# Inputs laid out in load order, and an eighth FFN slab pair by the seven-product scheme

## The chip, the core and the metric

The kernel runs on one core of one Trainium2 chip. The metric is the device time of one execution in microseconds, the median of several runs. The engines of the core are PE (TensorE; PEld is its weight load), DVE (VectorE), ACT (ScalarE), POOL (GpSimd) and SP (SyncE, which here only issues DMAs). All DMAs share 16 DMA engines.

## What is computed

Two transformer-like blocks in float32 over 256 tokens and a model width of 2048, one after the other. What matters here is the FFN of the second block:

```python
h = rmsnorm_2(x, ffn_norm_g[i])
hid = h @ w_ffn_in[i]                     # 2048 x (2*5632)
gate, up = hid[..., :FFN_HIDDEN], hid[..., FFN_HIDDEN:]
x = x + (jax.nn.silu(gate) * up) @ w_ffn_out[i]
ple = p[i] @ w_ple[i]
x = x + jax.nn.sigmoid(rmsnorm_2(x, ple_norm_g[i]) @ w_ple_gate[i]) * ple
```

Ahead of it stand the first block (projections `w_in`, two recurrent mixers, `w_out`, `w_pg`) and the second block's `w_in_2`, attention, spatial gating and merge. All of them are products of a 256-token activation with weights that are read once, some 400 MB in all.

## The kernel before

**Pieces.** Every weight is cut into slabs of 512 columns and every slab into pieces of 256 rows (`PK = 2` blocks of 128 rows), 512 KB each. A piece g goes through four steps: SP (or POOL) loads it to `raw` (or `ple`, below); ACT copies it to `whi` in the rounded type fp32r; DVE subtracts, `wlo = raw - whi`; PE multiplies. The result has close to float32 accuracy because PE does three products: whi with the high part of the activation, whi with the low part, wlo with the high part. A standard piece is 2 row blocks x 2 token tiles x 3 products = 12 matmuls of 128x512 (lines L1275 for whi, L1280 for wlo), gathered in the PSUM tensor `acc`. `whi` and `wlo` are rings of 4 pieces, so ACT may be at most 4 pieces ahead of PE, and DVE follows ACT. Each engine has its program written out in piece order; `between(g)` puts the small DVE steps behind the split of a certain piece.

**Seven products.** Some pairs of slabs (the gate slab and the up slab j of the FFN, and two pairs of the merge stage) are not done as 2 x 8 standard pieces but as a 2x2 block product over token halves, K halves and the two slabs, by a scheme with seven products M1 to M7 instead of eight. Such a pair is 7 x 4 = 28 pieces of 6 matmuls (L1646 for whi, L1650 for wlo, into `aux`). Its price is on the other engines: every piece is split by ACT (L1097) and DVE (L2458) as a standard one is, though PE works on it for half as long; and eight of the 28 pieces first need a sum of two weight blocks on DVE (`s_sum`, L2453). M5 and M4 need a sum with the four resident pieces of `r1` (in the trace `ple`), which POOL makes by an accumulating DMA (L830): for M5.q once DVE has split M1.q, for M4.q once it has split M6.q. Each block ends in some 512-wide DVE steps: `s_up`, `s_gates` (three), `s_hidden` (three).

**Blocks.** `BLOCKS` is a table: each row is one pair j by seven products, and the standard units that are mixed in (gate or up slabs, or `out`, a slab quarter of the product with `w_ffn_out`). The first two rows belong to the merge stage, the other seven to the FFN (j = 1, 2, 4, 5, 7, 8, 10), each with 16 standard pieces. `add_block` lays them out so that roughly two seven-product pieces stand between two standard ones. `M6.q, M7.q, M3.q` for q = 0 to 3 are in the middle, M4 at the end. `FILLS` says behind which standard piece PE transposes half of a finished hidden slab (4 transposes, L1723); ACT and DVE split it (L1184, L2575) three pieces later. After the last block there is a tail: 16 standard pieces for the hidden slabs 9 and 8, then four times `ple` and two pieces for slab 10, then the last product `gate2` with 32 pieces.

**Loads.** The weights stand in memory as rows of the whole matrix, so a 512-column slab comes in runs of 2 KB. Standard pieces come in pairs of 1 MB (L629, L726), in a seven-product block into two pairs of buffers that take turns: the load of a pair waits for DVE's split of the last piece that stood there. Four slots hold the half loads for the blocks b12, b21, b22 (L743). SP issues all of them in one order, sorted by when the buffer is free.

**Start.** The vectors of gains are loaded as rows and transposed by PE: 16 rows of `norm_w` first (L1298; then DVE copies them, L1856), the rest behind piece 8 (L1304, L1305). `p` and `p_2` (`ptok`, L1258) and the spatial weights `w_s_2` (L1527, from `att_z`) are transposed by PE too, 8 transposes each. PE begins with 8 + 4 throw-away products (`warm`, L1317), between them the first 8 transposes of x.

Of the kernel before, what the change touches and what calls it, by code (L numbers as in the profile page):

```python
# [29 lines left out]
F32 = mybir.dt.float32  # L30
# [68 lines left out]
FILLS = [(0, 2, 0, 0, "d"), (0, 5, 0, 1, "d"), (1, 2, 1, 0, "d"), (1, 5, 1, 1, "d"), (2, 3, 3, 0, "d"), (2, 6, 3, 1, "d"),  # L99
# [12 lines left out]
class Plan:  # L112
# [30 lines left out]
    def unit(self, role, j, q=0):  # L143

        if role == "out":
            return [(role, j, q + i, p) for h in range(2) for i in range(2) for p in (2 * h, 2 * h + 1)]
        return [(role, j, q, p) for p in range(4 if role in ("uA", "uB") else 8)]
# [28 lines left out]
    def plan_ffn(self):  # L176
# [7 lines left out]
        for c in range(M_GROUPS, S_GROUPS):  # L184
# [80 lines left out]
def plan_aux():  # L265

    names = [("gain0", 0)] + [("xT", i) for i in range(8)] + [("gains", 0)]
# [5 lines left out]
    names.extend([("p", 0), ("p2", 0)])  # L273
# [13 lines left out]
    two("tr2", 0); two("ws"); two("tr2", 1); two("tr2", 2)  # L287
# [15 lines left out]
def two_blocks_kernel(nc, A, out):  # L303
# [4 lines left out]
    with ctx:  # L308
# [136 lines left out]
        wsr = zt[:, :, :].rearrange("p a b -> p (a b)")[:, 0:1024].rearrange("p (g s) -> p g s", g=8)  # L445
# [18 lines left out]
        def view(w):  # L464
            return w.rearrange("(k p) n -> p k n", p=P)
# [18 lines left out]
        SHORT = {SLABS[n][0] for q in range(4) for n in (FIRST["DP"] + q, PLAN.ffn_slab["ple", 0, q])}  # L484
        out_k = lambda role, j, p: (4 * j + p * PK) if role == "out1" else 4 * j[p // 2] + p % 2 * PK

        def raw_piece(g):

            slot = PLAN.slot[g] if g >= PLAN.g_plan else g % RAW
            if g not in SHORT:  # L490
                return raw[:, slot]
            pair = raw[:, slot // 2 * 2:slot // 2 * 2 + 2].rearrange("p q k c -> p (q k c)")
            return pair.rearrange("p (k q c) -> p q k c", k=PK, q=2)[:, slot % 2]
# [29 lines left out]
        def s_weights(c, what, q):  # L523
# [31 lines left out]
        hid_of = lambda c: merge_h[c] if c < M_GROUPS else hid_s[c % 2]  # L555
# [63 lines left out]
        def _(sp):  # L619
            piece = [0]  # L620

            def load(src, i=0):
# [6 lines left out]
                sp.dma_start(dst.rearrange("p (k c) -> p k c", k=src.shape[1]), src).then_inc(raw_loaded[g // 2 % (RAW // 2)], 16)  # L629
# [2094 lines left out]
```

## Time and profile before

| | us |
|---|---|
| median of 3 runs (2007.98 to 2010.89) | 2008.88 |
| the profiled execution | 2009.09 |
| its span, from first to last instruction | 2007.4 |
| PE busy | 1997.2 (99%) |
| PE weight load busy | 1663.0 (83%) |
| DVE busy | 1452.3 (72%) |
| ACT busy | 1104.2 (55%) |
| POOL busy | 121.2 (6%) |

The profiled execution lasted 1.7 us longer than its span. Spans of matmuls overlap in the profile (each is shown at 0.39 us, the next begins after 0.23 us), so the share of PE says little by itself: how many matmuls start in a stretch says more. The granted clock is the full 2.4 GHz level throughout by the profile's row of it.

### The profile page before, as it was taken

What the parts mean: (1) busy time and instruction counts of PE and PEld (TensorE: products, weight loads), DVE (VectorE), ACT (ScalarE), POOL (GpSimd) and SP (SyncE); (2) the same over time, 40 slices, a digit from 0 to 9 for tenths busy, and PEclk for the clock granted to TensorE, in tenths of its full rate; (3) what the DMA queues carried; (4) which work ended last, traced back from release to release, by engine and by line L of the source; (5) the groups of instructions that cost most, each with busy time, mean ns of one, the idle gap of its engine ahead of it and who ended that gap; (6) DMA issues with size and microseconds to landing.
All of it is one profiled execution on the core that took longest, in us unless ns stands there. A gap on an engine that the chain in (4) does not pass through costs nothing.

```text
span 2007.4 us, 23490 instructions
## 1 busy us (share of the span) xinstructions
PE 1997.2 (99%) x9253; PEld 1663.0 (83%) x9253; DVE 1452.3 (72%) x1550; ACT 1104.2 (55%) x1373; POOL 121.2 (6%) x116
## 2 busy tenths in 40 slices
PE   9999999999999999999999999999999999999999
PEld 8888888888888888888888888888888888888887
DVE  6877676655666666768787656888888898887664
ACT  6545454554466456555655445656556565665553
POOL 1000000000001100001100000110001100010000
PEclk9999999999999999999999999999999999999999
DMA  8544454556556564558887656889988988887553
GB/s 286 169 146 160 134 181 155 189 188 207 184 184 202 185 211 160 182 195 233 261 231 245 214 189 210 226 252 257 271 257 227 265 243 265 271 227 217 181 194 126
DMA packets 214754, 420.60 MB, mean 210 GB/s; under 512 B 10690, under 2 KB 13428, under 8 KB 214260
## 3 DMA queue, kind: packets, MB, share of 16 engines
q1 hardware_dynamic: 195060, 381.35, 55.5%
q0 software_dynamic: 19584, 37.75, 11.2%
q8 instruction: 73, 1.20, 0.2%
q14 instruction: 37, 0.30, 0.0%
HBM read 414.35 MB, written 4.72 MB: 209 GB/s over the span
## 4 chain that ended last, share of the span: by engine, by line
PE 96%; DVE 1%; DMA 1%; ACT 1%; issue 0%; SPq 0%; DVEq 0%; ACTq 0%
PE acc L1275 48%; PE acc L1280 24%; PE aux L1646 11%; PE aux L1650 6%; PE aux L1258 2%; PE aux L1348 1%; DMA raw<-in_w_ffn_in 1%; DVE wlo L1794 1%; PE aux L1723 0%; ACT whi L858 0%; PE aux L1317 0%; PE aux L1338 0%; PE aux L1249 0%; PE aux L1363 0%; DVE att_z L2296 0%
## 5 line engine op out<-in xcount | busy, mean ns | idle before, releaser
L1794 DVE TENSOR_TENSOR wlo<-raw,whi 128x1024 fp32r<-128x1024 f32 x560 | 681.9, 1222 | 389.1 <-ACT whi L858 379.7
L858 ACT ACTIVATE whi<-raw 128x1024 fp32r<-128x1024 f32 x560 | 591.0, 1059 | 634.2 <-PE acc L1280 550.9
L1275 PE MATMUL acc<-whi,actA_hi 128*128 128x512 f32 x1024 | 404.1, 395 | 1.2 <-ACT whi L858 1.1
L1275 PE MATMUL acc<-whi,actA_lo 128*128 128x512 f32 x1024 | 398.9, 390 | 0.0
L1275 PE MATMUL acc<-whi,actB_hi 128*128 128x512 f32 x860 | 337.5, 392 | 0.0
L1275 PE MATMUL acc<-whi,actB_lo 128*128 128x512 f32 x860 | 334.7, 389 | 0.0
L1280 PE MATMUL acc<-wlo,actA_hi 128*128 128x512 f32 x1024 | 274.1, 389 | 0.0
L1280 PE MATMUL acc<-wlo,actB_hi 128*128 128x512 f32 x860 | 230.4, 390 | 0.7 <-DVE wlo L1794 0.6
L1275 PEld LDWEIGHTS acc<-whi,actA_hi 128*128 128x128 f32 x1024 | 192.3, 188 | 41.0 <-issue 1.6
L1280 PEld LDWEIGHTS acc<-wlo,actA_hi 128*128 128x128 f32 x1024 | 192.2, 188 | 40.3
L1275 PEld LDWEIGHTS acc<-whi,actA_lo 128*128 128x128 f32 x1024 | 192.4, 188 | 38.4
L1097 ACT ACTIVATE whi<-ple 128x1024 fp32r<-128x1024 f32 x144 | 151.2, 1058 | 94.3 <-PE acc L1280 76.4
L2458 DVE TENSOR_TENSOR wlo<-ple,whi 128x1024 fp32r<-128x1024 f32 x144 | 174.0, 1220 | 28.7 <-ACT whi L1097 26.5
L1280 PEld LDWEIGHTS acc<-wlo,actB_hi 128*128 128x128 f32 x860 | 161.3, 188 | 34.9 <-DVE wlo L1794 1.5
L1275 PEld LDWEIGHTS acc<-whi,actB_lo 128*128 128x128 f32 x860 | 161.6, 188 | 32.6
L1275 PEld LDWEIGHTS acc<-whi,actB_hi 128*128 128x128 f32 x860 | 161.5, 188 | 32.7
L1097 ACT ACTIVATE whi<-raw 128x1024 fp32r<-128x1024 f32 x108 | 114.1, 1061 | 88.4 <-PE acc L1280 69.2
L2458 DVE TENSOR_TENSOR wlo<-raw,whi 128x1024 fp32r<-128x1024 f32 x108 | 131.7, 1221 | 36.5 <-ACT whi L1097 33.9
L1646 PE MATMUL aux<-whi,actB_hi 128*128 128x512 f32 x272 | 106.4, 391 | 0.0
L1646 PE MATMUL aux<-whi,actB_lo 128*128 128x512 f32 x272 | 105.9, 389 | 0.0
L830 POOL DMA_DIRECT2D ple<-in_w_ffn_in x56 | 67.7, 1219 | 527.8 <-DVE wlo L2458 501.4
L832 POOL TENSOR_TENSOR rstd<-var,minus_half 128x8 f32<-128x8 f32 (+1 forms) x15 | 24.5, 1631 | 1048.5 <-DVE var L1825 1048.5
(342 smaller groups left out, 2318.6 us busy)
## 6 DMA issues: line engine op xcount, KB each, us to landing
raw<-in_w_in SPq DMA_DIRECT2D x116, 1024.0 KB, 5.0
raw<-in_w_ffn_out SPq DMA_DIRECT2D x44, 1024.0 KB, 7.1
raw<-in_w_ffn_in SPq DMA_DIRECT2D x84, 512.0 KB, 7.7
raw<-in_w_ffn_in SPq DMA_DIRECT2D x32, 1024.0 KB, 6.1
ple<-in_w_ffn_in POOLq DMA_DIRECT2D x56, 512.0 KB, 8.5
raw<-in_w_in SPq DMA_DIRECT2D x32, 512.0 KB, 7.6
raw<-in_w_out SPq DMA_DIRECT2D x16, 1024.0 KB, 4.9
raw<-in_w_pg SPq DMA_DIRECT2D x16, 1024.0 KB, 5.0
```

The costliest lines, as they stand in the source:

```text
L830: pool.dma_start(r1[:, q], s_weights(c, what, q), accum_op=ALU.add).then_inc(sem(f"r1_added{q}"), 16)
L832: pool.tensor_tensor(rstd[:, i, 0:n], var[:, i, 0:n], minus_half[:, 0:n], ALU.pow).then_inc(pow_out, 1)
L858: act.activation(whi[:, g % RING], raw_piece(g), ACT.Copy).then_inc(hi_ready, 1)
L1097: act.activation(whi[:, g % RING], s_source(c, m, q), ACT.Copy).then_inc(hi_ready, 1)
L1258: ins = pe.transpose(bank(u)[:, c * S + t * P:c * S + (t + 1) * P], src[:, t, (c0 + c) * P:(c0 + c + 1) * P], ident[:, :])
L1275: pe.matmul(acc2(n)[:, t, :], act[x][:, k + c, t * P:(t + 1) * P], whi[:, g % RING, c, :], start=(p == 0 and c == 0 and x == 0), stop=False)
L1280: ins = pe.matmul(acc2(n)[:, t, :], act[0][:, k + c, t * P:(t + 1) * P], wlo[:, g % RING, c, :], start=False, stop=(last and c == PK - 1))
L1348: ins = pe.matmul(bank(u)[:, j * m:(j + 1) * m], Kp[n % 2][:, c:c + P], Qp[n % 2][:, j * m:(j + 1) * m], start=True, stop=True)
L1646: pe.matmul(o, lhs(x, q * PK + k), whi[:, g % RING, k, :], start=(q == 0 and k == 0 and x == 0 and not onto), stop=False, skip_group_check ...
L1650: ins = pe.matmul(o, lhs(0, q * PK + k), wlo[:, g % RING, k, :], start=False, stop=(q == 3 and k == PK - 1), skip_group_check=onto)
L1794: dve.tensor_tensor(wlo[:, g % RING], raw_piece(g), whi[:, g % RING].bitcast(F32), ALU.subtract)\
L2458: dve.tensor_tensor(wlo[:, g % RING], s_source(c, m, q), whi[:, g % RING].bitcast(F32), ALU.subtract)\
```

## The change

Two parts. **Layout:** a function on the host, `_lay_out`, hands the weights over as blocks in load order (slab, half of K by 512 rows, partition, 4 row blocks, 512 columns), so that a 1 MB load has one run of 8 KB per partition and a half load one of 4 KB; it also hands over `p`, `p_2`, `w_s_2` and all vectors of gains already transposed, so that PE's transposes and DVE's copies of them go, and 13 small loads become one. **Plan:** the pair 9 is done by seven products as well, so there are eight FFN blocks (j = 1, 2, 4, 5, 7, 8, 9, 10). The standard pieces are dealt out anew: the blocks of 5, 7, 8 and 9 have 12 each instead of 16 (a unit may now be cut by `start` and `stop`), the others 16. The tail loses its 16 `out` pieces and has the four `ple` pieces first. A third hidden buffer, bank "a" for transposes, and waits that match them come with it.

```diff
-    (5, [("out", (3, 2), 0), ("out", (3, 2), 2)]),
-    (7, [("out", (6, 4), 0), ("out", (6, 4), 2)]),
-    (8, [("gate", 9), ("up", 9)]),
-    (10, [("out", (5, 7), 0), ("out", (5, 7), 2)]),
+    (5, [("out", (3, 2), 0), ("out", (3, 2), 2, 0, 4)]),
+    (7, [("out", (3, 2), 2, 4, 8), ("out", (6, 4), 0)]),
+    (8, [("out", (6, 4), 2), ("out", (5, 7), 0, 0, 4)]),
+    (9, [("out", (5, 7), 0, 4, 8), ("out", (5, 7), 2)]),
+    (10, [("out", (8, 9), 0), ("out", (8, 9), 2)]),
...
-        tail = self.unit("out", pair, 0) + self.unit("out", pair, 2) \
-            + [x for q in range(4) for x in (("ple", 0, q, 0), ("out1", last, q, 0), ("out1", last, q, 1))]
+        tail = [("ple", 0, q, 0) for q in range(4)] + [("out1", OUT_LAST, q, p) for q in range(4) for p in range(2)]
...
-        def view(w):
-            return w.rearrange("(k p) n -> p k n", p=P)
+        def chunks(w, c, k, n):
+
+            slab = c // COLS if w != "w_in" or c < MI else (c - HQ) // COLS + MI // COLS
+            return A[w][slab, k // 4, :, k % 4:k % 4 + n, :]
...
-            sp.dma_start(stage1[C_NORM:C_NORM + KD, :], A["norm_w"].rearrange("a (r c) -> (a r) c", c=P))\
-                .then_inc(sem("norm_loaded"), 16)
+            sp.dma_start(gains[:, C_NORM:C_NORM + KD], A["vectors"][:, C_NORM:C_NORM + KD]).then_inc(sem("norm_loaded"), 16)
...
-            pe.wait_ge(sem("norm_loaded"), 16)
-            pe.transpose(bank(0)[:, 0:KD], stage1[0:KD, :], ident[0:KD, 0:KD]).then_inc(aux_full, 1)
...
-                        transposes(("p", 0), ptok[0], 0)
-                        transposes(("p2", 0), ptok[1], 0)
...
-                    if (s, p) == (2, 1):
-                        spatial_weights()
...
-                    if r == "ple" and g == SLABS[m][-1] + 2:
+                    if r == "ple" and g == SLABS[m][-1] + 1:
                         ple_slab(m, x, ple2)
...
+    def blocks(w):
+        k, n = w.shape
+        return w.reshape(k // 512, 4, P, n // COLS, COLS).transpose(3, 0, 2, 1, 4)
```

In the whole program PE has 8944 matmul instructions instead of 8987. Those of 128x512 in split pieces go from 3072 on `acc` with `actA` to 2880, and from 1320 on `aux` to 1488: 24 fewer. 19 transposes go, 8 each of `ptok` and `att_z` and 3 of `stage`. The transposes of the hidden slabs are 88 in both.

At the start of PE's program the kernel before has:

```order
0 L1241 UNCONDITIONAL_BRANCH
1 L1298 MATMUL aux<-ident,stage 128x16
2 L1317 MATMUL aux<-ident 128x128 x8
3 L1258 MATMUL aux<-ident,resid 128x128 x8
4 L1317 MATMUL aux<-ident 128x128 x4
5 L1275 MATMUL acc<-whi,actA_hi 128x512
```

and the changed one:

```order
0 L1230 UNCONDITIONAL_BRANCH
1 L1296 MATMUL aux<-ident 128x128 x8
2 L1247 MATMUL aux<-ident,resid 128x128 x8
3 L1296 MATMUL aux<-ident 128x128 x4
4 L1264 MATMUL acc<-whi,actA_hi 128x512
```

The transpose of `stage`, which waits for the load of `norm_w`, no longer stands ahead of the throw-away products.

In the middle of the block of pair 5 (M6 to M3) the DVE program was as follows; `wlo<-raw` on L1794 is a standard piece, `wlo` on L2458 one of seven products (`ple` as source is M6, `raw` is M7 or M3), L2453 is a sum, L2620 adds a finished `out` slab to the residual:

```order
824 L2458 TENSOR_TENSOR wlo<-raw,whi 128x1024
825 L2453 TENSOR_TENSOR ple<-ple,raw 128x1024
826 L2458 TENSOR_TENSOR wlo<-raw,whi 128x1024
827 L2453 TENSOR_TENSOR raw<-raw 128x1024
828 L1794 TENSOR_TENSOR wlo<-raw,whi 128x1024
829 L2458 TENSOR_TENSOR wlo<-ple,whi 128x1024
830 L2458 TENSOR_TENSOR wlo<-raw,whi 128x1024
831 L2453 TENSOR_TENSOR ple<-ple,raw 128x1024
832 L1794 TENSOR_TENSOR wlo<-raw,whi 128x1024
833 L2458 TENSOR_TENSOR wlo<-raw,whi 128x1024
834 L2453 TENSOR_TENSOR raw<-raw 128x1024
835 L2458 TENSOR_TENSOR wlo<-ple,whi 128x1024
```

The same place in the changed kernel (its lines are L1762, L2416, L2411 and L2578 for the same four things):

```order
818 L2416 TENSOR_TENSOR wlo<-raw,whi 128x1024
819 L2411 TENSOR_TENSOR ple<-ple,raw 128x1024
820 L2416 TENSOR_TENSOR wlo<-raw,whi 128x1024
821 L2411 TENSOR_TENSOR raw<-raw 128x1024
822 L1762 TENSOR_TENSOR wlo<-raw,whi 128x1024
823 L2416 TENSOR_TENSOR wlo<-ple,whi 128x1024
824 L2416 TENSOR_TENSOR wlo<-raw,whi 128x1024
825 L2411 TENSOR_TENSOR ple<-ple,raw 128x1024
826 L2416 TENSOR_TENSOR wlo<-raw,whi 128x1024
827 L2411 TENSOR_TENSOR raw<-raw 128x1024
828 L2578 TENSOR_TENSOR resid<-resid,acc 128x2x512
829 L1762 TENSOR_TENSOR wlo<-raw,whi 128x1024
```

Between two standard pieces there stand now three seven-product pieces with two sums, where there stood two or three pieces with one or two sums; the addition to the residual has moved from between M6.0 and M3.0 to behind M3.1.

On PE, behind the last seven-product block, the kernel before goes on with `out` pieces, among which slab 10 is transposed, and then comes to `ple` (`p1T`). In the changed kernel the end of the block is followed by:

```order
6129 L1264 MATMUL acc<-whi,p1T_lo 128x512
6130 L1269 MATMUL acc<-wlo,p1T_hi 128x512 x4
6131 L1691 MATMUL aux<-ident,hid_std 128x128 x4
6132 L1264 MATMUL acc<-whi,p1T_hi 128x512
6133 L1264 MATMUL acc<-whi,p1T_lo 128x512
```

Slab 10 (`hid_std`) is transposed behind the second and the third `ple` piece, 4 transposes each; in the kernel before such a place among the `out` pieces of the tail was:

```order
6068 L1275 MATMUL acc<-whi,hidT_x_lo 128x512
6069 L1280 MATMUL acc<-wlo,hidT_x_hi 128x512 x4
6070 L1723 MATMUL aux<-ident,hid_s 128x128 x4
6071 L1275 MATMUL acc<-whi,hidT_x_hi 128x512
6072 L1275 MATMUL acc<-whi,hidT_x_lo 128x512
```

## Rows read from the trace of the kernel before

**Rows 1.** The page: busy time and the share of the last chain by engine.

```profile
PE 1997.2 (99%) x9253; PEld 1663.0 (83%) x9253; DVE 1452.3 (72%) x1550; ACT 1104.2 (55%) x1373; POOL 121.2 (6%) x116
...
PE 96%; DVE 1%; DMA 1%; ACT 1%; issue 0%; SPq 0%; DVEq 0%; ACTq 0%
```

**Rows 2.** Waits of PE: engine line waited for, us in total, times, longest.

```profile
PE aux L1298 <- DMA stage<-in_norm_w: 2.5, 1, 2.5
PE acc L1275 <- ACT whi L858: 1.1, 2, 0.9
```

**Rows 3.** PE over time in `gate2`: start, us, line, operation; one standard piece.

```profile
1937.10 0.39 PE L1275 MATMUL acc<-whi,actB_hi 128*128 128x512 f32 x1
...
1939.82 0.39 PE L1275 MATMUL acc<-whi,actB_hi 128*128 128x512 f32 x1
```

**Rows 4.** PE over time at `ptok`, and at the two transposes of gains.

```profile
49.18 1.03 PE L1258 MATMUL aux<-ident,ptok 128*128 128x128 f32 x8
49.98 0.48 PE L1275 MATMUL acc<-whi,actA_hi 128*128 128x512 f32 x1
50.29 0.40 PE L1275 MATMUL acc<-whi,actA_lo 128*128 128x512 f32 x1
```

```profile
36.88 0.27 PE L1304 MATMUL aux<-ident,stage 128*128 128x128 f32 x1
...
37.27 0.50 PE L1275 MATMUL acc<-whi,actA_hi 128*128 128x512 f32 x1
```

**Rows 5.** The start, all engines over time, up to the first product.

```profile
2.08 0.31 ACT L904 ACTIVATE junk<-ident 128x128 f32<-128x128 f32 x1
...
2.72 3.78 PE L1317 MATMUL aux<-ident 128*128 128x128 f32 x16
...
6.30 1.92 PE L1258 MATMUL aux<-ident,resid 128*128 128x128 f32 x8
...
8.21 1.06 ACT L858 ACTIVATE whi<-raw 128x1024 fp32r<-128x1024 f32 x1
...
9.41 0.47 PE L1275 MATMUL acc<-whi,actA_hi 128*128 128x512 f32 x1
```

**Rows 6.** PE where the first two FFN blocks begin; ACT where pair 5's begins.

```profile
1253.19 0.47 PE L1275 MATMUL acc<-whi,actA_hi 128*128 128x512 f32 x1 [0.88 <-ACT whi L858]
...
1341.69 0.50 PE L1275 MATMUL acc<-whi,actA_hi 128*128 128x512 f32 x1 [0.22 <-ACT whi L858]
```

```profile
1506.47 1.06 ACT L858 ACTIVATE whi<-raw 128x1024 fp32r<-128x1024 f32 x1 [5.93 <-DMA raw<-in_w_ffn_out]
```

**Rows 7.** Stretches: PE, PEld, DVE, ACT, POOL busy (instructions), granted clock, DMA share, GB/s.

```profile
1502.00:1585.00 83.00, 83.00 (x371) 68.73 (x370) 71.28 (x66) 49.48 (x51) 9.66 (x8) 1.00 0.89 259
```

**Rows 8.** DVE over time, block of pair 5: M6, M7, M3.

```profile
1536.03 1.22 DVE L2458 TENSOR_TENSOR wlo<-ple,whi 128x1024 fp32r<-128x1024 f32 x1
...
1547.38 1.22 DVE L2458 TENSOR_TENSOR wlo<-ple,whi 128x1024 fp32r<-128x1024 f32 x1
1548.52 1.22 DVE L2458 TENSOR_TENSOR wlo<-raw,whi 128x1024 fp32r<-128x1024 f32 x1
1551.03 1.23 DVE L2453 TENSOR_TENSOR ple<-ple,raw 128x1024 f32<-128x1024 f32 x1 [1.30 <-DMA raw<-in_w_ffn_in]
...
1555.58 1.22 DVE L2458 TENSOR_TENSOR wlo<-ple,whi 128x1024 fp32r<-128x1024 f32 x1
```

**Rows 9.** PE over time: the two wlo products of M6.2 in that block.

```profile
1557.79 0.61 PE L1650 MATMUL aux<-wlo,actB_hi 128*128 128x512 f32 x2
```

**Rows 10.** POOL over time in that block, and its eight DMAs to landing.

```profile
1513.63 2.45 POOL L830 DMA_DIRECT2D ple<-in_w_ffn_in  x2 [0.97 <-DVE wlo L2458]
```

```profile
DMA to landing us min/median/max: 5.8/8.5/15.5
```

**Rows 11.** The page: DMA queues, SP's (q1) and POOL's (q0); packets, MB, share of 16 engines' span.

```profile
q1 hardware_dynamic: 195060, 381.35, 55.5%
q0 software_dynamic: 19584, 37.75, 11.2%
```

More of the change, by code:

```diff
@@ L141, in __init__, with unit @@
             assert free < need
-    def unit(self, role, j, q=0):
+    def unit(self, role, j, q=0, start=0, stop=8):
         if role == "out":
-            return [(role, j, q + i, p) for h in range(2) for i in range(2) for p in (2 * h, 2 * h + 1)]
+            return [(role, j, q + i, p) for h in range(2) for i in range(2) for p in (2 * h, 2 * h + 1)][start:stop]
         return [(role, j, q, p) for p in range(4 if role in ("uA", "uB") else 8)]
@@ L265, in plan_aux @@
 def plan_aux():
-    names = [("gain0", 0)] + [("xT", i) for i in range(8)] + [("gains", 0)]
+    names = [("xT", i) for i in range(8)]
     def two(name, *key):
@@ L348, in two_blocks_kernel @@
         rs = ExitStack()
-        stage1 = sb("stage1", [P, P], at=rs)
-        stage2 = sb("stage2", [C_END - P, P], at=rs)
-        ptok = [sb(f"ptok{n}", [P, T, PE_DIM], at=rs) for n in range(2)]
+        sb("fill_stage", [P, 256], at=rs)
+        p_raw = [sb(f"p_raw{n}", [P, PK, S], at=rs) for n in range(2)]
         rs.close()
@@ L489, in raw_piece @@
             slot = PLAN.slot[g] if g >= PLAN.g_plan else g % RAW
[L490 to L493, printed above, removed]
+            return raw[:, slot]
         S_SRC = {"M1": None, "M2": "b21", "M5": None, "M6": None, "M7": "b12", "M3": "b22", "M4": None}
@@ L526, in s_weights @@
             w, col = s_columns(c, 0 if what in ("b11", "b21") else 1)
-            return view(w[0])[:, k:k + PK, col:col + COLS]
+            return chunks(w, col, k, PK)
         def s_columns(c, half):
             j = BLOCKS[c][0] * COLS
-            return (A["w_in_2"], (GA2, GB2)[half] + j) if c < M_GROUPS else (A["w_ffn_in_2"], (FFN, 0)[half] + j)
+            return ("w_in_2", (GA2, GB2)[half] + j) if c < M_GROUPS else ("w_ffn_in_2", (FFN, 0)[half] + j)
         def s_done(eng, c, m):
@@ L577, in filled, with fill_place @@
             eng.wait_ge(sem("tr_taken"), 1 + [x[2:4] for x in FILLS].index((j, h)))
+        def fill_place(f):
+            c, _, _, _, b = FILLS[f]
+            return 2 if b == "d" else 3 - own(c)
         def fill_bank(f):
-            c, _, _, _, b = FILLS[f]
-            return aux[:, 2 if b == "d" else 3 - own(c), :].rearrange("p (c s) -> p c s", c=2)
+            return aux[:, fill_place(f), :].rearrange("p (c s) -> p c s", c=2)
         def fill_dst(x, f):
@@ L1715, in fill @@
                 else:
-                    pe.wait_ge(sem("tr_taken"), f)
+                    same = [x for x in range(f) if fill_place(x) == fill_place(f)]
+                    if same:
+                        pe.wait_ge(sem("tr_taken"), same[-1] + 1)
                 if b == "e":
                     pe.wait_ge(sem("s_up"), c + 1)
+                elif b == "a":
+                    pe.wait_ge(sem("hid_odd_ready"), c)
                 else:
@@ L2629, in between @@
                 for (role, j, q), n in PLAN.ffn_slab.items():
-                    if role == "out" and j != OUT_TAIL[0] and g == SLABS[n][-1] + (2 if SLABS[n][-1] in PLAN.block_end else 3):
+                    if role == "out" and g == SLABS[n][-1] + (2 if SLABS[n][-1] in PLAN.block_end else 3):
                         out_added(n, q)
```

155 lines of the change are left out of this document (65 added, 90 removed), and 6 rows, old and new, of the table FILLS.

## The prediction

> **What bounds the kernel now.** I read the page first: PE is busy 99% of the span and is 96% of the chain that ended last [rows 1]. Such a share can hide gaps, so I looked at PE's waits: apart from the first, they come to some 2 us [rows 2]. Where nothing but standard pieces run, a piece starts every 2.72 us, 226.7 ns for each of its 12 matmuls [rows 3]; nearly the whole span has that spacing. So PE's instructions are the time: what leaves PE is gained, unless the others fall behind. DVE's 72% is an average; in the FFN blocks it is 71.28 of 83 us, and the DMA engines are at 0.89 [rows 7]. There the slack is small, and the change makes exactly this part denser.
>
> **Matmuls.** The instruction lists have 24 fewer matmuls of 128x512: 192 go (16 standard pieces), 168 come (28 pieces of 6). 24 x 0.2267 = **-5.44 us** on the path.
>
> **Transposes.** Eight of `ptok` start at 49.18, the next matmul at 49.98 and its successor 0.31 later instead of 0.23 [rows 4]: 0.80 + 0.08, say 0.9 us. The eight of `att_z` are of the same shape: 0.9. The two of gains take 0.39 up to the next matmul [rows 4], with the same 0.1 behind: 0.5. Sum **-2.3 us**. What goes with them on DVE and ACT lay under PE's work and gives nothing. The masking of the spatial weights stays on POOL, and they are needed seven slabs later.
>
> **Start.** PE's first instruction waits 2.5 us for the load of `norm_w` [rows 2]; then come the throw-away products, and the x transposes start behind them without a gap [rows 5]. The identity was ready by 2.08, when ACT read it [rows 5]; ACT had just loaded its table, so it may have been ready some tenths earlier. Without the wait PE can begin 0.6 to 1.0 us earlier, and the chain transposes, ACT, DVE, first product at 9.41 [rows 5] moves along as far as x and the first weights have landed. Bounds: 0 if one of these is late, -1.0 if none is. ACT took up the first weights at 8.21 with no wait in its row, so I take **-0.8**.
>
> **Loads.** One run of 8 KB instead of four of 2 KB. The trace has no weight load in such runs, so the gain in rate is at least nothing; from above nothing bounds it, and I take 5%. It matters in two ways. At the start of the first FFN block PE stood 0.88 us for a late load and at that of the second 0.22 [rows 6]; both should mostly go: **-1.0** (bounds 0 and -1.4, the two with their slower restart). And it pays for the denser blocks: a copy costs 0.555 x 16 x 2007.4 / 381.35 = 46.7 engine-us per MB, 2.9 us on 16 engines, an accumulation 0.112 x 16 x 2007.4 / 37.75 = 95, or 6.0 us [rows 11]. A block of 16 standard pieces has 32 copies and 8 accumulations of 0.524 MB, 49 + 25 = 74 us of 83, which is the 0.89 of [rows 7]. A block of 12 has 28 copies: 43 + 25 = 68 us in 28 x 1.36 + 12 x 2.72 = 71 us: 0.95 at the old rates, 0.92 if copies are 5% faster.
>
> The Trainium skill speaks against a gain in rate ("DMA: Bandwidth & Descriptors", Specifications): 512 B are enough for line rate, and the old runs are four times that. By it the term -1.0 would be 0 and the 0.95 would hold; that is the second case below. No run here shows yet which is right.
>
> **The four dense blocks (pairs 5, 7, 8, 9).** On average DVE keeps up: 40 splits + 8 sums + up to 2 additions to the residual, at 1.135 us from start to start (1547.38, 1548.52 in [rows 8]) are 57 us, some nine or ten 512-wide steps at about 0.7 another 6: 63 of 71. But in the middle (M6 to M3) three seven-product pieces and one standard piece are 3 x 1.36 + 2.72 = 6.80 us of PE and 4 splits + 2 sums = 6.81 us of DVE: no slack at all for four rounds. Before, that stretch had 1.33 standard pieces a round: 7.7 us of PE against 7.2 of DVE. DVE lives there on the lead that it brings. In the block of pair 5 the split of M6.2 ended at 1555.58 + 1.22 = 1556.80, PE wanted it at 1557.79 [rows 8, 9]: a lead of 1.0 us, after an idle 1.3 us for a half load. The order of DVE up to M6.2 stays nearly the same, so the dense block arrives there with about the same lead, and now two rounds without recovery follow, with the addition to the residual (1.135 us) behind M3.1 in the blocks of 5 and 8; those of 7 and 9 have none between M6.0 and M7.3. I get some 1.0 us of PE standing in block 5, 0.6 in block 8 (a split of transposes more, but PE's own transposes too), about none in 7 and 9.
>
> Second, the sums for M5 come by accumulating DMAs. The last of block 5 was issued near 1514.9 and landed 15.5 us later, at 1530.4; DVE split M5.3 at 1536.03, ACT 1.1 us before [rows 8, 10]. So it had 4.5 us to spare; from M1.3 to M5.3 a dense block is 5.44 us of PE shorter (16.32 for 21.76). DVE then waits about 1 us and brings less lead to M6. That costs another 0.2 to 0.5 us a block. Third, at every block's beginning the third standard piece waits for its load: ACT stood 5.93 us for it and went on at 1506.47 [rows 6], just in time. This distance stays 8.16 us of PE or more, so 0 to 0.3 a block. Together **+2.5 us**, bounds 0 and 7. The blocks of 1, 2, 4 and 10 keep the old density and cost nothing new.
>
> **Tail.** 16 pieces that gave DVE a rest go; slab 10 is transposed behind the second and third `ple` piece, 5 us after its block, when DVE's hidden step (three 512-wide operations, some 2 us) is done. The split of its second half may be some 0.2 us late; that lies inside the bounds above.
>
> **Sum.** 2009.09 - 5.44 - 2.3 - 0.8 - 1.0 + 2.5 = 2002.05 for an execution like the profiled one; that one stood 0.2 above the median of the runs, so **2001.9 us**.
>
> **The rivals.**
> 1. *The layout gives no rate.* Then -1.0 goes, and in the dense blocks the DMA engines stand at 0.95. For it: 259 GB/s with a share of 0.89 [rows 7] tells of accumulations, not of short runs. Against it: fewer, longer packets. Price: +1.0, and about 1 us more in each dense block: 2001.9 + 1 + 4 = 2007. Chance 0.12.
> 2. *Slower: accumulations starve in the dense blocks.* Both queues share the 16 engines; if a turn of SP's queue carries up to four times the bytes of before, POOL's gets a smaller part. Place: M5.3. From the split of M1.3 (3.8 us ahead of PE by the order of the pieces) to PE's need are 16.3 + 3.8 us; ACT and DVE take 2.3, which leaves 17.8 for the DMA, now up to 15.8 with its wait. It decides from there: landing at 21.3 stops PE 3.5 us in every dense block and leaves DVE no lead for the middle, which is worth 1.5 more: 4 x 5 = 20 in place of 2.5, some 2019. Against it: the four accumulations have few copies beside them that are not needed anyway. Chance 0.06.
>    The Trainium skill (same page, "Queues, rings and completion order") has the engines take turns between queues packet by packet; by it this shift is possible, and no row of the kernel before can show it.
> 3. *DVE never runs out*, and the start gives its full 1.0: 2009.09 - 5.44 - 2.3 - 1.0 - 1.0 - 0.2 = 1999.2. It is the good end of the forecast.
> 4. *The change does not do what it says*: the dense blocks are bound by DVE, so that the 5.44 are eaten. Against it: 63 of 71 us on average; it would take stops of over 1.4 us in each of them beyond what I counted: 2007 to 2009. Chance 0.05.
>
> **How the numbers follow.** Forecast 0.75 (1999.2 to 2004.8, with the good end), rival 1 0.12, rival 2 0.06, rival 4 0.05, something else 0.02. A measurement of this kernel can tell about 0.2%, 4.0 us, from no change: faster is below 2004.9, slower above 2012.9. Faster 0.77, same 0.16, slower 0.07. The range leaves out rival 2 and the far parts of 1 and 4: 1999.0 to 2007.0.
>
> **What would show it.** Right: in the profile after, 43 fewer PE instructions, the first product near 8.6, matmuls 226.7 ns apart outside the dense blocks, PE's waits of 1 to 2 us in the middle of the blocks of 5 and 8 with DVE `wlo` as the releaser, no wait at the start of the first FFN block, SP's queue below 55.5% of the span. Wrong: PE waits for `ple` loads at M5 or M4 (rival 2), a DMA share of 0.95 in the dense blocks (rival 1), PE waits in all four of them (rival 4), or first weights that land after 8.5.

## The result, and the profile after

The changed kernel takes 2013.44 us (median of 20 runs, 2009.77 to 2017.07), the kernel before 2009.62 (20 runs): ratio 1.0021, 95% interval 1.0015 to 1.0027. It is slower by 0.2% (3.8 us) where the prediction said 2001.9 and faster. The profiled execution took 2013.15, its span is 2011.6 against 2007.4.

From the page of the changed kernel, the rows that answer to [rows 1] and [rows 11]:

```profile
PE 1994.4 (99%) x9210; PEld 1655.0 (82%) x9210; DVE 1473.1 (73%) x1569; ACT 1115.5 (55%) x1386; POOL 103.5 (5%) x124
...
q1 hardware_dynamic: 66080, 381.35, 51.7%
q0 software_dynamic: 11520, 41.95, 12.0%
...
PE 85%; DMA 6%; DVE 6%; ACT 1%; issue 1%; SPq 0%; ACTq 0%; DVEq 0%
```

43 PE instructions fewer, as the lists said, and SP's queue needs less of the DMA engines. But PE's share of the last chain fell from 96% to 85%: DMAs and DVE now end it, each for 6%. PE's waits (engine line waited for, us in total, times, longest), which answer to [rows 2]:

```profile
PE aux L1614 <- DVE wlo L2416: 3.2, 3, 1.3
PE acc L1264 <- ACT whi L846: 2.6, 3, 1.7
PE acc L1269 <- DVE wlo L1762: 2.3, 3, 0.8
```

**Where they are.** The 1.7 is the start's, one 1.3 stands at 954 us, a 0.6 at 809 was there before; nearly all the rest is in the four dense blocks or right behind them. The last matmul of the program ended in the kernel before at 2002.16 + 0.39, its first product of the block of pair 5 began at 1502.48; in the changed kernel:

```profile
1501.64 0.39 PE L1264 MATMUL acc<-whi,hidT_x_hi 128*128 128x512 f32 x1
```

```profile
2006.24 0.39 PE L1280 MATMUL acc<-wlo,actB_hi 128*128 128x512 f32 x1
```

Up to the block of pair 5 the changed kernel is 0.84 us ahead (1502.48 - 1501.64). From there to PE's end it needs 504.99 us where the other needed 500.07. With 24 matmuls fewer it should be 494.6, so it loses **10.4 us** there. I had put 2.5. Counted from the trace as what the starts of neighbouring matmuls are apart over the usual 0.23 us, some 5.5 of it stand in the middle of the four blocks, 1.7 at M4.3, 1.7 at the third standard piece of the next block and 0.5 at the start of `gate2`, where PE waits 0.17 us for DVE's split of the activation; the rest is short gaps.

**The first kind of stop**, DVE in the middle of the block of pair 5, where [rows 8, 9] showed a lead of 1.0 us:

```profile
1545.01 1.23 DVE L2411 TENSOR_TENSOR ple<-ple,raw 128x1024 f32<-128x1024 f32 x1 [1.18 <-DMA raw<-in_w_ffn_in]
1546.15 1.22 DVE L2416 TENSOR_TENSOR wlo<-raw,whi 128x1024 fp32r<-128x1024 f32 x1
1547.29 1.22 DVE L2411 TENSOR_TENSOR raw<-raw 128x1024 f32<-128x1024 f32 x1
1548.42 1.22 DVE L2578 TENSOR_TENSOR resid<-resid,acc 128x1024 f32<-128x1024 f32 x1
1549.55 1.22 DVE L1762 TENSOR_TENSOR wlo<-raw,whi 128x1024 fp32r<-128x1024 f32 x1
```

```profile
1550.83 1.21 PE L1269 MATMUL acc<-wlo,hidT_x_hi 128*128 128x512 f32 x4 [0.84 <-DVE wlo L1762]
```

DVE waits 1.18 us for a half load, works without a gap behind it, and PE stands when the split of 1549.55 is not there in time. There is no slack between two standard pieces, so nothing makes the wait good: what it and the addition to the residual (1.13 us) come to beyond DVE's lead, PE stands. In the block of pair 7 there is no addition, and the half loads alone do it (DVE waits 0.71 us for one and 2.63 for the next):

```profile
1628.28 1.23 DVE L2411 TENSOR_TENSOR ple<-ple,raw 128x1024 f32<-128x1024 f32 x1 [2.63 <-DMA raw<-in_w_ffn_in]
```

```profile
1630.69 0.50 PE L1614 MATMUL aux<-wlo,actB_hi 128*128 128x512 f32 x1 [1.11 <-DVE wlo L2416]
```

The block of 8 has a half-load wait of 1.37 us, that of 9 two of 1.28 and 1.79. In the kernel before, each block had one such wait of 1.30 to 1.37 us and one of 0.4 or less, and PE stood behind none of them. **The second kind** closes the block. ACT at M4.3 and at the third standard piece of the next block, and the chain of work through the first of them (start, us, what):

```profile
1569.27 1.06 ACT L1086 ACTIVATE whi<-ple 128x1024 fp32r<-128x1024 f32 x1 [4.81 <-DMA ple<-in_w_ffn_in]
...
1579.02 1.06 ACT L846 ACTIVATE whi<-raw 128x1024 fp32r<-128x1024 f32 x1 [4.62 <-DMA raw<-in_w_ffn_out]
```

```profile
1559.38 9.87 DMA ple<-in_w_ffn_in
1569.25 0.02 issue
1569.27 1.07 ACT whi L1086
1570.34 0.02 issue
1570.36 1.24 DVE wlo L2416
1571.60 0.04 issue
1571.64 0.73 PE aux L1614 x2
```

The accumulating DMA for M4.3 can start only when DVE has split M6.3. It took 9.87 us, and PE followed at once. ACT waits for this DMA in all four dense blocks; PE stops for it in those of 5 and 7, in the second trace (e11) also in that of 9.

**DVE and the DMA engines over a dense block** (PE, PEld, DVE, ACT, POOL busy, granted clock, DMA share, GB/s), which answers to [rows 7]:

```profile
1502.00:1575.00 73.00, 71.77 (x313) 57.82 (x312) 63.19 (x59) 43.91 (x45) 6.90 (x8) 1.00 0.83 247
```

DVE's 63.19 us are what I had counted (63 of 71), and the DMA share did not rise to 0.92: it fell to 0.83. Neither average was the bound.

### The profile page after: what moved, and what is told of

Same layout as the page of the kernel before. It is cut to its first block, busy times and chain, and to the rows that moved or that the text cites. A ratio compares the mean times of both kernels' runs of the same rounds, so it can differ in the third digit from the quotient of the medians.

```text
span 2011.6 us, 23458 instructions
## 1 busy us (share of the span) xinstructions
PE 1994.4 (99%) x9210; PEld 1655.0 (82%) x9210; DVE 1473.1 (73%) x1569; ACT 1115.5 (55%) x1386; POOL 103.5 (5%) x124
## 3 DMA queue, kind: packets, MB, share of 16 engines
q1 hardware_dynamic: 66080, 381.35, 51.7%
## 4 chain that ended last, share of the span: by engine, by line
PE 85%; DMA 6%; DVE 6%; ACT 1%; issue 1%; SPq 0%; ACTq 0%; DVEq 0%
PE acc L1264 45%; PE acc L1269 22%; PE aux L1610 9%; PE aux L1614 4%; DVE wlo L2416 2%; DMA raw<-in_w_ffn_in 2%; DMA ple<-in_w_ffn_in 2%; PE aux L1247 2%; PE aux L1327 1%; DVE wlo L1762 1%; DMA raw<-in_w_ffn_out 1%; DMA raw<-in_w_in 1%; DVE ple L2411 1%; DVE raw L2411 1%; ACT whi L1086 0%
## 5 line engine op out<-in xcount | busy, mean ns | idle before, releaser
L1762 DVE TENSOR_TENSOR wlo<-raw,whi 128x1024 fp32r<-128x1024 f32 x544 | 662.8, 1223 | 399.5 <-ACT whi L846 391.7
L1264 PE MATMUL acc<-whi,actA_hi 128*128 128x512 f32 x960 | 379.3, 395 | 1.7 <-ACT whi L846 1.7
L1264 PE MATMUL acc<-whi,actA_lo 128*128 128x512 f32 x960 | 374.7, 390 | 0.0
L1269 PE MATMUL acc<-wlo,actA_hi 128*128 128x512 f32 x960 | 257.4, 390 | 0.0
L1086 ACT ACTIVATE whi<-ple 128x1024 fp32r<-128x1024 f32 x160 | 167.2, 1058 | 99.9 <-PE acc L1269 54.2
L2416 DVE TENSOR_TENSOR wlo<-ple,whi 128x1024 fp32r<-128x1024 f32 x160 | 193.3, 1221 | 27.4 <-ACT whi L1086 25.3
L1264 PEld LDWEIGHTS acc<-whi,actA_hi 128*128 128x128 f32 x960 | 180.6, 188 | 38.5 <-issue 2.2
L2416 DVE TENSOR_TENSOR wlo<-raw,whi 128x1024 fp32r<-128x1024 f32 x120 | 145.9, 1221 | 24.7 <-ACT whi L1086 22.0
L1610 PE MATMUL aux<-whi,actB_hi 128*128 128x512 f32 x304 | 119.0, 391 | 0.0
L1610 PE MATMUL aux<-whi,actB_lo 128*128 128x512 f32 x304 | 118.3, 389 | 0.0
L1614 PE MATMUL aux<-wlo,actB_hi 128*128 128x512 f32 x304 | 94.2, 391 | 2.1 <-DVE wlo L2416 1.9
L818 POOL DMA_DIRECT2D ple<-in_w_ffn_in x64 | 55.3, 864 | 586.9 <-DVE wlo L2416 564.5
```

The lines of the kernel that those rows point to most:

```text
L818: pool.dma_start(r1[:, q], s_weights(c, what, q), accum_op=ALU.add).then_inc(sem(f"r1_added{q}"), 16)
L1086: act.activation(whi[:, g % RING], s_source(c, m, q), ACT.Copy).then_inc(hi_ready, 1)
L1264: pe.matmul(acc2(n)[:, t, :], act[x][:, k + c, t * P:(t + 1) * P], whi[:, g % RING, c, :], start=(p == 0 and c == 0 and x == 0), stop=False)
L1269: ins = pe.matmul(acc2(n)[:, t, :], act[0][:, k + c, t * P:(t + 1) * P], wlo[:, g % RING, c, :], start=False, stop=(last and c == PK - 1))
L1610: pe.matmul(o, lhs(x, q * PK + k), whi[:, g % RING, k, :], start=(q == 0 and k == 0 and x == 0 and not onto), stop=False, skip_group_check ...
L1614: ins = pe.matmul(o, lhs(0, q * PK + k), wlo[:, g % RING, k, :], start=False, stop=(q == 3 and k == PK - 1), skip_group_check=onto)
```

## Experiments

The base is the changed kernel unless said otherwise. "Over 494.6" is the stretch from the first product of the block of pair 5 to PE's end, less the 494.6 us that its matmuls and transposes need; it comes from one trace of each kernel, the ratios from 5 to 11 executions of each against the kernel before. It is more than the sum of the waits that the profile names, since PE starts again more slowly (from 1549.59 to 1550.83 above are 1.24 us, 1.01 more than the usual 0.23, for a wait of 0.84), and it holds a stretch at half clock in e4 and three in e6 (last section). The profiled executions of e1 and e9 have one more right behind their first product. e4 and e8 leave out a part of the computation, as their texts say.

| kernel | ratio, 95% | over 494.6 |
|---|---|---|
| changed kernel | 1.0021 (1.0015 to 1.0027) | 10.4; again: 14.8 |
| e1 layout, old plan | 0.9988 (0.9979 to 0.9997) | (old plan) |
| e2 plan, old layout | 1.0018 (1.0010 to 1.0027) | 7.1 |
| e3 dense blocks spread anew | 0.9974 (0.9966 to 0.9983) | 4.8 |
| e4 no sums on DVE | 0.9986 (0.9977 to 0.9995) | 8.2 |
| e5 as e3, first slab in 2 KB runs | 0.9978 (0.9969 to 0.9986) | 6.4 |
| e6 as e3, spread otherwise | 1.0038 (1.0025 to 1.0050) | 17.2 |
| e7 as e3, all inputs in the old layout | 0.9981 (0.9973 to 0.9990) | 3.4 |
| e8 plain copies on POOL's queue | 0.9996 (0.9987 to 1.0006) | 9.2 |
| e9 as e3, weights in 2 KB runs | 0.9969 (0.9956 to 0.9981) | 1.5 |
| e10 as e3, middle as before | 0.9996 (0.9987 to 1.0005) | 6.0 |

**e1 and e2: the two parts apart.** e1 is the diff without its hunks on `BLOCKS`, `FILLS`, `HID_T`, the tail and the transposes' banks; e2 is those hunks alone.

> The new layout and the transposed inputs with the plan of before (seven FFN blocks of 16 standard pieces, 16 out pieces in the tail). Theory A, the plan makes the stops: the blocks of 16 run without stops as before, the 19 transposes (-2.3) and part of the late loads (-0.5 to -1.0) are gained, and the one new stop at 954 (1.5 us, a half load that landed 3.2 us later than before) may come back: 2006 to 2008, ratio 0.998 to 0.999. Theory B, runs of 4 and 8 KB make the half loads and the accumulations land later wherever both queues are busy: stops of 1 us or more appear in the old blocks too, time 2010 or more, ratio 1.000 to 1.003.

> The new plan (eight FFN blocks, four of them with 12 standard pieces) with the inputs as before in runs of 2 KB. Theory A: 24 matmuls less (-5.4), but the stops of the four dense blocks stay at 9 us or grow, since the DMA engines carry the same bytes: 2013 to 2016, ratio 1.001 to 1.003. Theory B: the dense blocks stop for 2.5 us or less as they should have by my count: 2005 to 2008, ratio 0.998 to 0.999.

e1: 2007.44 us, e2: 2013.33, before 2009.53. So the plan alone is as slow as the whole change (theory A): its own four dense blocks stop wherever the inputs lie, and the blocks of 16 in e1 have no stop of over 0.2 us. But the layout, worth 0.12% by itself, brought nothing that shows on top of the plan (1.0018 and 1.0021, each known to some 0.1%), although 19 transposes went with it. So something of it may cost in the dense blocks what the transposes gave.

**e3: deal the 12 pieces out anew.**

```diff
-            upto = max(0, min(28, (t - 1) * 28 // (len(std) - 3)))
+            upto = (0, 3, 6, 9, 12, 14, 16, 19, 21, 24, 28, 28)[t] if len(std) == 12 else max(0, min(28, (t - 1) * 28 // (len(std) - 3)))
```

> The changed kernel with the 12 standard pieces of a dense block dealt out otherwise: behind the 2nd one come three seven-product pieces at once (before: behind the 3rd), and one more stands between M6 and M3. Theory A1, stops come where the pieces of PE are too short for DVE (M6 to M3) and where four standard pieces in a row share two pairs of buffers (the block's beginning): the stops of the four blocks fall from 9.4 us to 3 or less, 2005 to 2008. Theory A2, the accumulating DMAs for M4.3 and M5.3 are the bound, since they land 0.02 us before ACT takes them: these two places are as far from their source as before, so the stops only move there, 2011 to 2014.

2004.12 us: seven changed table entries are worth 0.47%, 9.4 us, and the kernel beats both. The same work, DMAs and bytes are there. PE's waits in it (the first row is the start's 2.4 and one of 0.7 at a block's beginning; the 0.7 of the second stands in the middle of the block of 9, behind a half load that DVE waited 3.29 us for):

```profile
PE acc L1264 <- ACT whi L846: 3.1, 2, 2.4
PE aux L1614 <- DVE wlo L2416: 0.7, 1, 0.7
PE aux L1610 <- ACT whi L1086: 0.5, 1, 0.5
```

**e10 parts e3's two moves.** `(0, 3, 6, 9, 12, 15, 18, 21, 24, 26, 28, 28)`. It is not e3's first move alone: M6.3 to M4.3 has two standard pieces here, where e3 and the changed kernel have one.

> The kernel of e3 without its additional standard piece between M6 and M3 (every third place again, as in the changed kernel); it now stands between M4.1 and M4.2, and three pieces are still behind the 2nd at the block's beginning. Theory A1 (between M6 and M3 PE's time is too short for DVE's): the stops at M3.1 or M3.2 of all four blocks come back, 1 us or more each, 2008 to 2011. Rival (only the rows of standard pieces at the block's edge and M4.3 matter): 2003 to 2005.

2007.78 us, ratio 0.9996, just below what A1 expected. PE stands again for DVE's `wlo` in the middle, by 0.8 us at most, and in this trace in the blocks of 5 and 8 alone, the two with the addition to the residual; A1 had said all four and 1 us or more (a 0.6 of the first row is the old one at 809):

```profile
PE acc L1269 <- DVE wlo L1762: 2.6, 4, 0.8
PE aux L1614 <- DVE wlo L2416: 0.7, 2, 0.5
```

So the piece between M6 and M3, against one between M4.1 and M4.2, is worth 0.22% (0.9996 to 0.9974), some 4.4 us, and the block's edges (M4.3, the third standard piece) 0.25% (1.0021 to 0.9996), some 5 us. The second figure holds two things that no run parts: the row of standard pieces at a block's beginning is shorter, and M4.3 stands 2.7 us further from M6.3. PE stops for neither in this trace. The two shares are of about the same size; each interval is some 0.1% wide to either side.

**e6: one move too many.** `(0, 0, 3, 6, 9, 12, 14, 17, 20, 23, 26, 28)`.

> The kernel of e3 with one more change in the dense blocks: the last but one standard piece stands between M4.1 and M4.2 and none behind M4.3, so that M4.3 is 2.7 us further from M6.3, whose split frees its place for the accumulating DMA (three standard pieces then stand in a row at a block's beginning). In e3 M4.3's sum landed 0.02 us before ACT took it in three of four dense blocks. Theory A2 for the rest of e3's stops (1.1, 0.4 us at M4.3 in blocks 5 and 7): these go, some 2002 to 2003. Rival: the three in a row bring back the late third load (1 us per block) and nothing is won, 2004 to 2007.

2017.58 us, slower than everything, where I had expected 2002 to 2007, and by neither mechanism that I had named. DVE and PE in the block of pair 5:

```profile
1546.65 1.22 DVE L2411 TENSOR_TENSOR ple<-ple,raw 128x1024 f32<-128x1024 f32 x1 [3.67 <-DMA raw<-in_w_ffn_in]
```

```profile
1550.19 1.25 PE L1269 MATMUL acc<-wlo,hidT_x_hi 128*128 128x512 f32 x4 [2.62 <-DVE wlo L1762]
```

Here no standard piece stands between M3.0 and M7.1. The slot of b22 is freed by the split of M3.0 and must be full again for the sum of M6.2, which DVE does right behind M7.1. That is a loop with a load in it: 7.1 us from issue (1539.52) to landing (1546.63) for three DVE steps of 1.14 us. In e3 and in the changed kernel one standard piece stands there, and in the changed kernel the wait was 1.18 us. This third mechanism, the reuse of the four half slots, bounds the middle from the load's side as DVE's work does from the other. It is not e6's alone: DVE's half-load waits in the four dense blocks come to 9.2 us in the changed kernel, and each of its stops in the middle stands behind one.

**e4 and e8: take DVE's or the DMA engines' work away.** e4 replaces `tensor_tensor` in `s_sum` by a bare `sem_inc` in the dense blocks; e8 drops `accum_op=ALU.add` from POOL's DMAs.

> The changed kernel without DVE's sums of weight blocks (s_sum) in the four dense blocks, so 8 x 1.14 us less DVE work in each; this part of the computation is left out. Every wait for the half loads stays. If DVE's work is the bound there (A1): no waits for wlo in the middle, and M4.3 is free earlier too, stops 2 us or less, 2005 to 2007. If the transfers are (A2): DVE has spare time but ACT still stands for ple at M4.3 and for raw at the third standard piece, stops of 4 us or more, 2009 to 2012.

> The changed kernel with POOL's DMAs in all blocks as plain copies without the addition, so that each costs the DMA engines about half; the addition of these weight blocks is left out. DVE's and PE's work and every wait stay. Theory A2 (transfers bind the dense blocks, DVE's lag at M6 to M3 comes from late half loads and a late M5.3): the stops fall from 9.4 us to 3 or less, 2005 to 2007. Theory A1 (too little PE time for DVE's work between M6 and M3, and the row of standard pieces at a block's beginning): only M4.3's stops go, 2010 to 2012.

e4: 2007.02, e8: 2008.76 us. Each gives back 5 to 7 us of the change's loss, neither all of it. 9 us less DVE work per block goes mostly into longer waits for half loads: some 23 us in the four blocks instead of 9.2, once 6.96, behind which PE stood 2.96. And DMAs that land 1 to 4 us sooner still leave short stops in the middle (0.4 us at most) and the late third piece (1.97 and 1.29). e4 came out at the edge of A1's range and e8 between the two. So A1 and A2 both hold in part, and the half slots are the third cause.

**e7 and e9: what the layout is worth under the good plan.** e7 is e2 with e3's table. e9 is e3 with the weight matrices as they were:

```diff
-            slab = c // COLS if w != "w_in" or c < MI else (c - HQ) // COLS + MI // COLS
-            return A[w][slab, k // 4, :, k % 4:k % 4 + n, :]
+            return A[w].rearrange("(k p) n -> p k n", p=P)[:, k:k + n, c:c + COLS]
```

> New plan, dense blocks spread as in e3, inputs in the old layout with runs of 2 KB and PE's 19 transposes. Against e3 it tells what the layout is worth where the plan is the same: if the sum of my terms holds (2.3 for the transposes, 1.0 to 1.5 for the first FFN blocks' late loads, the start nothing), e3 + 3 to 4 us: 2007 to 2008. If dense blocks need the faster transfers on top (rival 1 of the prediction), their stops come back and it is 2010 or more.

> The kernel of e3 (new plan, dense blocks spread anew, p, w_s and the gains handed over transposed), but the weight matrices as before, in runs of 2 KB. It parts the layout in two. Theory L1, the runs of 4 and 8 KB win nothing and cost something (late half loads at 954 in the changed kernel and at 1550 in e5, first weights 1.2 us later, accumulations 0.5 to 1.3 us later): the late loads at the first FFN blocks come back (+1) but the start is 0.7 earlier and dense blocks stop for 2 us as in e7 in place of 3.4: 2002.5 to 2004, no slower than e3. Theory L2, long runs are worth 1 us or more: 2005 to 2006.

e7: 2005.35, below both theories (2007 to 2008; 2010 or more), and e9: 2003.91 us (6 runs), the lowest median of all, as L1 had it, though not to be told from e3. From e7 to e9 only the small inputs and the start change: 0.12%, 2.4 us, which agrees with the 2.3 of the prediction, but the two intervals overlap. From e9 to e3 only the runs of the weights change, and nothing is won (0.9969 against 0.9974, inside the intervals). The stretch 1242 to 1250 suggests why. SP's loads for the first FFN block stand in a row there and nothing else moves. Columns as above, the kernel before, the changed kernel, e9:

```profile
1242.00:1250.00 8.00, 8.00 (x37) 6.64 (x36) 4.63 (x4) 1.34 (x2) 0.00 (x0) 1.00 1.05 406
```

```profile
1242.00:1250.00 8.00, 8.00 (x37) 6.64 (x36) 4.63 (x4) 2.16 (x3) 0.00 (x0) 1.00 0.97 378
```

```profile
1242.00:1250.00 8.00, 8.00 (x37) 6.60 (x37) 4.63 (x4) 2.79 (x3) 0.00 (x0) 1.00 1.05 409
```

Five traces with 2 KB runs have 406 to 409 GB/s in this stretch, nine with runs of 4 and 8 KB have 362 to 401. Over the whole span the long runs cost the engines less time per byte (51.7% for 55.5%), and yet no more bytes move where loads stand in a row. The share is lower there too (0.97 for 1.05), so per busy time the rate is the same (390 and 387); why the engines stand idle a little in this row with long runs, no run tells. The times to landing in the page's list of DMA issues (KB each, median us) say the same, of the kernel before and of the changed one:

```profile
raw<-in_w_ffn_in SPq DMA_DIRECT2D x84, 512.0 KB, 7.7
raw<-in_w_ffn_in SPq DMA_DIRECT2D x32, 1024.0 KB, 6.1
ple<-in_w_ffn_in POOLq DMA_DIRECT2D x56, 512.0 KB, 8.5
```

```profile
raw<-in_w_ffn_in SPq DMA_DIRECT2D x96, 512.0 KB, 8.6
ple<-in_w_ffn_in POOLq DMA_DIRECT2D x64, 512.0 KB, 9.7
raw<-in_w_ffn_in SPq DMA_DIRECT2D x24, 1024.0 KB, 7.2
```

These two kernels differ in the plan as well. With the plan the same, the medians for 512 KB, the accumulations and 1 MB go from 7.7, 8.1 and 5.8 (e9) to 8.4, 9.1 and 7.3 (e3), from 7.8, 8.1 and 5.9 (e2) to the changed kernel's 8.6, 9.7 and 7.2, and under the old plan from 7.7, 8.5 and 6.1 to 7.8, 9.0 and 7.2 (e1). So under the new plan the loads on which a dense block hangs came 0.7 to 1.6 us later by the layout, in the median. What that costs shows in the traces alone (over 494.6: e7 and e9 3.4 and 1.5, e3 and e5 4.8 and 6.4; e2 7.1, the changed kernel 10.4 and 14.8); the timed ratios of these kernels lie within each other's intervals. The late half load at 954 in the changed kernel may be of this kind (it took 10.2 us; in the kernel before 6.2), but e11 has no stop there:

```profile
953.46 1.23 DVE L2411 TENSOR_TENSOR ple<-ple,raw 128x1024 f32<-128x1024 f32 x1 [2.70 <-DMA raw<-in_w_in]
```

The Trainium skill ("DMA: Bandwidth & Descriptors", Specifications) has 512 B suffice for the line rate. The rate in the stretch above agrees: four times as long a run gave no more.

**e5: the start.**

```diff
-                    sp.dma_start(raw[:, g], chunks("w_in", A_COLS[0], g * PK, PK))\
+                    sp.dma_start(raw[:, g], A["w_first"].rearrange("k p c -> p k c")[:, g * PK:(g + 1) * PK, :])\
```

> The kernel of e3 (new layout, dense blocks spread anew) with the first slab alone in runs of 2 KB as before. Theory S1, the start lost what the removed wait gave because the first weights come later in runs of 4 KB (they landed at 8.15, 9.12, 8.64 and 8.77 us in the four profiles with the new layout, at 7.48 and 6.80 in the two with the old one): the first piece lands at 7.5 or earlier, the first product stands at 8.3 to 9.0 (e3: 9.86), 2003 to 2004. Theory S2, it is the order of the loads or the 128 pieces of 64 B for the gains: the first piece lands past 8 us again and nothing changes.

The first piece landed at 7.71, a little later than S1's 7.5, and the first product began at 8.94, as S1 had it; the time, 2004.45, is e3's. But e9, also with 2 KB runs there, had its first piece at 8.80. Over all traces the first piece landed at 6.80 to 8.41 with the old start (4 traces) and at 7.42 to 9.20 with the new (10 traces). One trace of each can't tell S1 from chance; what makes the new start later is left open.

**e11 and e12: the two kernels once more.**

> The changed kernel once more, for a second trace. Stops that the plan makes stand again at the same places: M3.1 or M3.2 of all four dense blocks with DVE wlo as releaser, and M4.3 or the third standard piece behind them. The stop at 954 and the stretch at half clock at 302 may be gone, if they are chance.

> The kernel before once more, for a second trace. If the stretch at half clock at 302 is nothing that the change made, it may be seen here too (26 of 33 timed executions of this kernel have a mean clock below 1.000, so I expect it), and the stops at 1251 and 1341 stand again.

e11 (2014.78 us) has all the dense blocks' stops again, larger, and none at 954. The biggest is 2.27 us for `wlo` at M3.1:

```profile
1547.00 0.73 PE L1614 MATMUL aux<-wlo,actB_hi 128*128 128x512 f32 x2 [2.27 <-DVE wlo L2416]
```

e12 (2010.29 us) has the stop at 1254 (0.82 us for `whi`), none at 1341, and the stretch at half clock, told of below.

## Why the prediction was wrong

The step that failed is **"the four dense blocks: +2.5 us, bounds 0 and 7"**. It measured 10.4 and 14.8 in two traces, and dealing the pieces out anew (e3) alone gave back 9.4 us of the time. The places that I named were right in part, the middle of the block with DVE `wlo` as the releaser. But one cause of the stops there, the half loads, had no term at all. Four things were wrong:

- *Blocks 7 and 9 were set to nothing, since they have no addition to the residual.* All four stop, 7 by 1.11 us and 9 by 0.82. With 6.80 us of PE against 6.81 of DVE there is nothing from which a lead could come back, so DVE's waits for half loads add up with the addition, and in 7 and 9 they are enough without it (0.71 and 2.63; 1.28 and 1.79 us). I had the 1.30 us wait of [rows 8] before me and took it as spent. The dense block also shortens the loop from the split that frees a half slot to the sum that needs it, which I never worked out.
- *The late accumulation was looked for at M5.3.* M5.3 landed 0.02 to 0.46 us before ACT took it and stopped nothing. It was M4.3. Between M6.3 and M4.3 the dense block has one standard piece where the old had two: 11.3 us of PE (1559.06 to 1570.38) in place of 14.1, for a DMA of 9.9 and DVE's lag. I had worked out this distance for M1.3 to M5.3 alone; that the last DMA before M5.3 took 15.5 us in [rows 10] but 13.3 here helped as well.
- *The third standard piece was given 0 to 0.3 a block.* Its load waits behind DVE, and when M4.3 is late it is late as well: ACT stood 4.6 to 6.1 us for it and PE up to 0.6, in e11 0.9.
- *The layout was to pay for the density*; under the new plan it made the loads later by 0.7 to 1.6 us.

None of the rivals describes the result by itself. Rival 4's sign (PE waits in all four blocks; 2007 to 2009, chance 0.05) came true, but DVE stood there for loads too and was not the only bound. Rival 1's premise came true (no rate from the layout; 2007, 0.12), its sign did not: the DMA share in the dense block was 0.83 and not 0.95. I had priced the two only one at a time. Rival 2's place, M5.3, did not stop PE, but its sign "M5 or M4" came in small, 0.28 and 0.17 us at M4.3, and its direction was right: the accumulations landed a median of 1.2 us later (8.5 to 9.7), and by 0.5 to 1.6 where only the layout differs.

The other terms:

- **Matmuls -5.44**: right. e9 needs 496.15 us for the stretch that took 500.07, so 3.9 of the 5.4 arrived, and its short gaps, none with a wait of over 0.2 us, account for the 1.5.
- **Transposes -2.3**: right. In the changed kernel the distance to the kernel before grows by 1.4 us behind `ptok` and the gains and by 0.9 behind `att_z`; e7 to e9 gives 2.4.
- **Start -0.8**: wrong. ACT's row of the first weights had no wait in [rows 5], but they had landed only 0.7 us before it. Now they end the wait:

```profile
8.17 1.06 ACT L846 ACTIVATE whi<-raw 128x1024 fp32r<-128x1024 f32 x1 [1.13 <-DMA raw<-in_w_in]
```

```profile
9.37 0.47 PE L1264 MATMUL acc<-whi,actA_hi 128*128 128x512 f32 x1 [1.73 <-ACT whi L846]
```

  The first product stood at 9.37, and in ten traces with the new start at 9.7 on average, where the old start's four have 9.4. The term is 0 to +0.3, and more where the clock falls: in e1 and e9 PE stood 3.30 and 2.07 us ahead of its first product, and a stretch at half clock followed within 1.3 us of it. The tell "first weights that land after 8.5" came true in six of the ten, not in the trace of the changed kernel (8.15).
- **Loads at the first FFN blocks -1.0**: the direction was right (-1.7 here, beyond the bound of -1.4, since both stops of [rows 6] are gone; the second is back with 0.77 us in e11), the reason was not. e9, with runs of 2 KB, has no stop at the first block either, while e2, e7 and e12 have one of 0.7 to 0.8. The four with it have the old small inputs and the others the new. Why, no run tells.
- **Tail, inside the bounds**: right. No stop stands at the transposes of slab 10; the 0.5 us at `gate2` are the only loss behind the last block.
- **Half clock, +1.6 in the profiled execution**: not in the sum. This stretch is not the change's doing, as e12 has it too; whether the changed kernel has more of them is open (below).

Added up: 0 - 2.3 - 1.7 + 1.6 (half clock) + 1.6 (half load at 954) - 5.4 + 10.4 = +4.2, the difference of the spans. The timed difference of the medians is 3.8.

## What to carry to other kernels

Where two engines' work per round is equal to within a tenth of a microsecond, price the round by its loops and not by its averages: for each buffer, the PE time from the piece that frees it to the piece that needs it, against the DMA's time to landing plus the work of the engines that follow. Check every such distance that the change shortens, not the one that was tight before. Then move the cover before giving up the saving: the same 12 pieces at other places turned +0.2% into -0.3%.

## What the runs showed of the hardware

- **Longer runs, less engine time, no more bytes.** With 8 KB and 4 KB in place of 2 KB SP's queue took 51.7% instead of 55.5% of the engines' span for the same 381.35 MB (e3 against e9, one plan: 52.1% and 55.4%), while loads landed later (e3 against e9, 1 MB: 7.3 for 5.8 us, 512 KB: 8.4 for 7.7) and the rate where loads stand in a row fell from 406 to 378 GB/s. The share of busy time is no measure of how soon a load lands.
- **Short stretches at half clock.** In the changed kernel the matmuls from 301.85 on are 0.43 us apart instead of 0.23, eight in a row, which costs 1.6 us. Columns as above; the changed kernel, and the kernel before in e12:

```profile
302.00:305.20 3.20, 3.20 (x10) 2.49 (x9) 3.17 (x10) 0.00 (x0) 0.00 (x0) 0.52 0.90 312
```

```profile
304.00:307.20 3.20, 3.20 (x9) 2.52 (x8) 3.01 (x10) 0.00 (x0) 0.00 (x0) 0.51 0.95 321
```

  0.5 is the lower level, 1.2 GHz. Just before, PE has four small transposes and eight products with four rows in place of whole ones:

```profile
298.80 0.41 PE L1379 MATMUL aux<-ident,hrow 4*128 4x4 f32 x4
299.06 1.97 PE L1386 MATMUL aux<-hrow,sel 4*128 4x256 f32 x8
```

  Each of the two kernels has this stretch in one of its two traces, and eight of all fourteen traces have it. In e6 half clock also followed stops: behind the one of 3.05 us for `wlo` at 1777.55 the clock was at the lower level:

```profile
1777.80:1781.00 3.20, 3.20 (x8) 2.55 (x9) 3.20 (x4) 1.20 (x2) 0.00 (x0) 0.50 0.35 120
```

  In e6 the three stops of 2.62, 2.71 and 3.05 us were followed by some 1.6, 1.3 and 2.4 us of such loss, over half as much again, which is part of why e6 is 13 us slower than e3. In e4 it followed a stop of 2.96 us; behind those of 2.27 in e11 and 2.33 in e5 it did not. Of the timed executions of the changed kernel 10 of 20 have a mean clock of 0.998, of the kernel before none of the 76 of which the clock is on record (55 at 0.999, 21 at 1.000). The changed kernel's ten have a median of 2014.3 us, its other ten 2012.7. So some of its loss may be clock; e2, with the plan alone, has no execution at 0.998 and is as slow.
